# Expert weights of an MoE decoder block: pairs of ring slots filled by one load of 4 MB, and w_down split by another order of its rows

## The chip, the cores and the metric

The kernel runs on one core of a Trainium2 chip. The metric is the device time in microseconds, the median of several runs. Everything is float32.

## The reference

One decoder block over 256 tokens of width 1024. A mixer (causal pooling and sliding-window attention, each with a sigmoid gate) is followed by a mixture of experts, which takes most of the time:

```python
logits = (t @ w_router + b_router)
top_vals, top_idx = lax.top_k(logits, TOP_K)                  # 4 of 32 experts
gates = einsum('tk,tke->te', softmax(top_vals), one_hot(top_idx, 32))
for e in range(32):                                           # w_up[e]: 1024 x 2048, w_down[e]: 1024 x 1024
    hu = t @ w_up[e] + b_up[e]
    glu, lin = minimum(hu[..., ::2], 7), clip(hu[..., 1::2], -7, 7)
    act = glu * sigmoid(1.702 * glu) * (lin + 1)
    out = out + gates[:, e:e+1] * (act @ w_down[e] + b_down[e])
```

The result is x plus mixer plus experts, and one last RMSNorm. All experts are read: 32 x (8 MB + 4 MB) of weights.

## The kernel before

**Passes.** Experts are taken in pairs, 16 passes of two experts each. A pass gathers up to 64 tokens for each of its two experts by a matmul with a 0/1 matrix (`gather`, line 724, in two halves), scales them (VectorE, `copy_xg`), multiplies by w_up (line 774), applies the clamped swiglu in four pieces j of 256 columns (VectorE and ScalarE), turns the result `hid` on TensorE so that its feature dimension lies on partitions (`turn_hid`, line 761, in halves m = 0 and 1, each copied by ScalarE, `copy_hidT`, line 499), multiplies by w_down (line 819) and scatters the rows back with the gates (line 855). Overfull experts would be served by further passes at the end; there are none with these inputs.

**The ring.** All large weights pass through `ring`, ten slots of 2 MB (16 KB on each of 128 partitions). The mixer fills the first 11 places (`MIXER_LOADS`); each pass has 12 loads. Loads 0 to 7 are w_up: load 2*kk+e holds, for expert e, input features p*8+2*kk and p*8+2*kk+1 on partition p, so two matmul steps k. Loads 8 to 11 are w_down: load 8+2*m+e holds rows m*512 to m*512+511 of expert e, row m*512+p*4+c on partition p. TensorE waits for a load when it needs it (`slot_load`, line 867) and takes the kk steps in order; for kk = 0 to 2 all four output pieces j are accumulated in each step, for kk = 3 the pieces are finished one after another, so that the swiglu of piece 0 begins while TensorE is still at piece 1.

**The queue of loads.** SyncE issues all of these loads, in the order of need, one after another (lines 341 to 346). Ahead of each it waits until the slot is free (`wait_freed`, line 328): TensorE has finished the step that read the load ten places earlier. In pass 0 the first ten loads wait for the last unit of the mixer that reads the slot (`last_use`, line 326). In the last pass the last two loads are cut otherwise (by output column, into six smaller DMAs) so that the end of w_down can begin sooner.

**Order on TensorE around the turn** (`pe_pass`, line 770). After the last up matmul: `turn_hid(g, 0)`, which waits for pieces 0 and 1 of `hid`; `gather(g + 1, 0)` for the next pass; the wait for the copy of the turn; the first half of w_down (k = 0 to 3); `turn_hid(g, 1)`; `gather(g + 1, 1)`; the second half (k = 4 to 7); the bias rows of the next pass; the scatter.

Of the kernel before, what the change touches and what calls it, by code (L numbers as in the profile page):

```python
# [15 lines left out]
P = 128  # L16
D = 1024
SEQ = 256
TT = SEQ // P
KD = D // P  # L20
# [15 lines left out]
PASSES = E // 2  # L36
ROUNDS = SEQ // SLOTS - 1
LISTED = 16
NJ, CH = 4, 512
# [14 lines left out]
KK, MH = 4, 2  # L54
UP_LOADS = 2 * KK
LOADS = UP_LOADS + 2 * MH
ALL_LOADS = MIXER_LOADS + PASSES * LOADS

# [36 lines left out]
def hybrid_block_kernel(nc, x, norm1_g, w_in, pool_w, pool_scale, w_pool_proj, sinks, w_attn_proj,  # L95
# [9 lines left out]
    with ExitStack() as ctx:  # L105
# [152 lines left out]
        def load_at(n):  # L258

            return full[n % R], LANDED * (n // R + 1)  # L260
# [3 lines left out]

        def slot_of(load):

            return (MIXER_LOADS + load) % R

        block = ctx.enter_context(nc.Block())

# [2 lines left out]
        def _(sp):  # L273
# [6 lines left out]
                sp.dma_start(ring[:, n % R, :].rearrange("p (k n) -> p k n", n=D),  # L280
                             src.rearrange("(k p) n -> p k n", p=P)).then_inc(full[n % R], LANDED)

            def load_expert(slot, load, pair, split=False):

                dst = ring[:, slot, :]
                if load < UP_LOADS:
                    kk, e = load // 2, load % 2
                    src = w_up_d[bass.ds(pair * 2 + e, 1)].rearrange("e (p k) n -> p (e k n)", p=P)
                    sp.dma_start(dst, src[:, kk * SLOT:(kk + 1) * SLOT]).then_inc(full[slot], LANDED)
                elif not split or load < LOADS - 2:  # L290
                    m, e = (load - UP_LOADS) // 2, load % 2
                    src = w_down_d[bass.ds(pair * 2 + e, 1), m * CH:(m + 1) * CH, :].rearrange("e (p k) n -> p (e k n)", p=P)
                    sp.dma_start(dst, src).then_inc(full[slot], LANDED)  # L293
                else:

                    n = load - (LOADS - 2)
                    src = w_down_d[pair * 2:pair * 2 + 2, CH:2 * CH, n * CH:(n + 1) * CH].rearrange("e (p k) n -> p e k n", p=P)
                    dst = dst.rearrange("p (e k n) -> p e k n", e=2, n=CH)
                    parts = [slice(0, 4)] if n == 0 else [slice(0, 2), slice(2, 4)]
                    for i, ks in enumerate(parts):  # L300
                        for e in range(2):
                            sp.dma_start(dst[:, e, ks, :], src[:, e, ks, :]).then_inc(tail_landed[n + i], 16)

            for t in range(TT):
                sp.dma_start(acc[:, t, :], x_d[t]).then_inc(x_loaded[t], 16)
# [11 lines left out]
            for j in range(NJ):  # L317
# [10 lines left out]
            def wait_freed(g, load):  # L328

                back = load - R  # L330
# [10 lines left out]
            for g in range(PASSES):  # L341
                for load in range(LOADS):
                    if g == 0 and load < R:
                        sp.wait_ge(unit_done, UNIT[last_use[load]] + 1)
                    else:
                        wait_freed(g, load)
                    load_expert(slot_of(g * LOADS + load), load, g, split=(g == PASSES - 1))

            sp.wait_ge(extra_ready, 1)
            extras = sp.value_load(n_extra[0:1, 0:1], min_val=0, max_val=LISTED)  # L350
            with sp.If(extras > 0):
                with sp.Fori(0, extras) as t:
                    pair = sp.value_load(x_pair[0:1, bass.ds(t, 1)], min_val=0, max_val=PASSES - 1)
                    for load in range(LOADS):
                        if load < R:
                            sp.wait_ge(down_done, (t + PASSES) * MH)
                        else:
                            sp.wait_ge(up_done, (t + PASSES) * (KK - 1) + 1)
                        load_expert((ALL_LOADS + load - LOADS) % R, load, pair)
            with sp.Else():  # L360
                pass

# [178 lines left out]
        def _(pe):  # L541
# [218 lines left out]

            def turn_hid(g, m):

                pe.wait_ge(hid_ready, g * NJ + 2 * (m + 1))
                if m >= 1:
                    pe.wait_ge(hidT_copied, g * MH + m)
                for c in range(4):
                    ins = nc.tensor.transpose(turn_bank[:, c * P:(c + 1) * P], hid[:, m * CH + c:(m + 1) * CH:4], ident[:, :])  # L767
                ins.then_inc(hidT_done, 1)

            def pe_pass(g, slot_load, following, split, first):  # L770
# [6 lines left out]
                    return ins  # L777

                for kk in range(KK):
                    w = [slot_load(2 * kk + e) for e in range(2)]  # L780
# [42 lines left out]
                w = [slot_load(UP_LOADS + e).rearrange("p (k n) -> p k n", k=4) for e in range(2)]  # L823
                for k in range(4):
                    for n in range(2):
                        ins = down(k, n, [w[e][:, k, n * CH:(n + 1) * CH] for e in range(2)])
# [4 lines left out]
                    gather(g + 1, 1, gather_bank)  # L831
                pe.wait_ge(hidT_copied, g * MH + 2)
                if not split:
                    w = [slot_load(UP_LOADS + 2 + e).rearrange("p (k n) -> p k n", k=4) for e in range(2)]
                for n in range(2):
                    if split:
                        last = ring[:, slot_of(g * LOADS + LOADS - 2 + n), :].rearrange("p (e k n) -> p e k n", e=2, n=CH)
# [26 lines left out]

            def main_load(g):

                def slot_load(load):
                    pe.wait_ge(*load_at(MIXER_LOADS + g * LOADS + load))
                    return ring[:, slot_of(g * LOADS + load), :]
                return slot_load  # L870

            for g in range(PASSES):
# [4 lines left out]
            extra_slots = [(ALL_LOADS + load - LOADS) % R for load in range(LOADS)]  # L877
            with pe.If(extras > 0):
                with pe.Fori(0, extras) as t:
                    def slot_load(load):  # L880
                        slot = extra_slots[load]

                        landed = sum(n % R == slot for n in range(ALL_LOADS - 2))
                        pe.wait_ge(full[slot], t * (LANDED * extra_slots.count(slot))
                                   + LANDED * (landed + extra_slots[:load + 1].count(slot)))
# [338 lines left out]
```

## Time and profile before

| | |
|---|---|
| median of 3 runs | 1134.2 us (1133.84 to 1134.38) |
| profiled execution, its own time | 1135.42 us |
| its span, first to last instruction | 1133.6 us |
| TensorE matmul busy | 1027.0 us (91%) |
| VectorE, ScalarE busy | 251.0 us (22%), 102.4 us (9%) |
| granted TensorE clock, mean | 0.974 |
| moved by DMA | 431.55 MB, mean 381 GB/s |
| loads of w_up | 128 of 2048 KB, median 36.8 us from issue to landing |
| loads of w_down | 62 of 2048 KB, 36.8 us; in the last pass 2 of 1024 KB and 4 of 512 KB |

The DMA engines' rate is given in slices of the span. Times from issue to landing hold the time in the queue. The mixer ends at about 203 us; the rest is the 16 passes. Offsets in the trace are microseconds from the span's start.

### The profile page before, as it was taken

How to read it: one execution, taken by the hardware profiler on the slowest of the kernel's cores; microseconds unless marked ns; L12 is line 12 of the kernel's file. 1: busy time of each engine (PE TensorE's matmuls, PEld its weight loads, DVE VectorE, ACT ScalarE, POOL GpSimd, SP SyncE). 2: the span in 40 equal slices, each digit the busy share in tenths (PEclk: the TensorE clock that was granted, in tenths of full speed). 3: DMA queues.
4: the chain of work that ended last, by engine and by line, in shares of the span. 5: the costliest groups of instructions: out<-in, count | busy, mean ns of one | idle time of the engine just before them, and what ended most of it. 6: DMA issues, size and time to landing. Idle time of an engine off the chain costs nothing.

```text
span 1133.6 us, 11141 instructions
## 1 busy us (share of the span) xinstructions
PE 1027.0 (91%) x4831; PEld 480.8 (42%) x4831; DVE 251.0 (22%) x561; ACT 102.4 (9%) x226; POOL 8.9 (1%) x20
## 2 busy tenths in 40 slices
PE   5499999999999998989898998898998989898986
PEld 4388874543434342424242434243434333333332
DVE  2032112331313211203031212121212121212112
ACT  1032011200101000001010101000000000000002
POOL 1200000000000000000000000000000000000000
PEclk9799999899999999999999999999999999999999
DMA  8760794699999999999999999999999999999994
GB/s 246 199 230 1 263 429 171 264 429 427 427 428 427 428 428 426 428 430 427 428 427 429 425 429 428 426 430 427 426 430 426 427 429 427 428 428 426 429 422 173
DMA packets 43302, 431.55 MB, mean 381 GB/s; under 512 B 5479, under 2 KB 7196, under 8 KB 18932
## 3 DMA queue, kind: packets, MB, share of 16 engines
q1 hardware_dynamic: 39992, 427.58, 89.7%
q0 software_dynamic: 976, 2.63, 1.4%
q10 hardware_dynamic: 2284, 0.60, 0.2%
q8 instruction: 40, 0.66, 0.2%
q14 instruction: 10, 0.08, 0.0%
HBM read 428.17 MB, written 2.62 MB: 380 GB/s over the span
## 4 chain that ended last, share of the span: by engine, by line
PE 51%; DMA 47%; DVE 1%; SPq 1%; issue 0%; ACT 0%; DVEq 0%; ACTq 0%
DMA ring<-in_w_down 32%; PE bank L774 15%; PE bank L819 15%; DMA ring<-in_w_up 11%; PE bank L572 9%; DMA ring<-in_w_in 4%; PE bank L729 3%; PE bank L855 3%; PE bank L675 3%; PE bank L767 1%; PE bank L758 1%; PE bank L692 0%; PE bank L589 0%; SPq L293 0%; PE bank L615 0%
## 5 line engine op out<-in xcount | busy, mean ns | idle before, releaser
L774 PE MATMUL bank<-ring,z_buf 128*64 128x512 f32 x2048 | 466.8, 610 | 51.0 <-issue 28.0
L774 PEld LDWEIGHTS bank<-ring,z_buf 128*64 128x64 f32 x2048 | 155.6, 140 | 347.7 <-issue 347.7
L819 PE MATMUL bank<-ring,m_buf 128*64 128x512 f32 x1024 | 226.8, 595 | 9.7 <-DMA ring<-in_w_down 9.0
L819 PEld LDWEIGHTS bank<-ring,m_buf 128*64 128x64 f32 x1024 | 78.1, 137 | 135.3 <-issue 132.7
L572 PE MATMUL bank<-h_buf,ring 128*128 128x256 f32 x400 | 91.5, 385 | 16.5 <-DMA ring<-in_w_in 15.6
L1116 DVE TENSOR_SCALAR swi<-bank 128x256 f32<-128x256 f32 x64 | 27.2, 425 | 311.9 <-PE bank L774 306.9
L572 PEld LDWEIGHTS bank<-h_buf,ring 128*128 128x128 f32 x400 | 76.7, 193 | 28.0 <-DMA ring<-in_w_in 16.1
L729 PE MATMUL bank<-u_buf,h_buf 128*128 128x128 f32 x512 | 64.5, 281 | 0.1
L729 PEld LDWEIGHTS bank<-u_buf,h_buf 128*128 128x128 f32 x512 | 62.1, 198 | 0.2 <-issue 0.2
L510 ACT ACTIVATE swi<-swi 128x256 f32<-128x256 f32 x64 | 26.7, 417 | 389.1 <-DVE swi L1116 389.1
L855 PE MATMUL bank<-y,u_buf 128*128 128x512 f32 x128 | 59.2, 605 | 0.0
L1087 DVE TENSOR_TENSOR z_buf<-bank,g2x 128x512 f32<-128x512 f32 x32 | 22.1, 692 | 148.5 <-PE bank L729 148.5
L1092 DVE TENSOR_TENSOR acc<-acc,bank 128x512 f32<-128x512 f32 x64 | 44.0, 687 | 30.0 <-PE bank L855 30.0
L855 PEld LDWEIGHTS bank<-y,u_buf 128*128 128x128 f32 x128 | 23.0, 189 | 35.1 <-issue 35.1
L1127 DVE COPY y<-bank 128x512 f32<-128x512 f32 x16 | 11.1, 692 | 113.8 <-PE bank L819 113.8
L501 ACT COPY m_buf<-bank 128x512 f32<-128x512 f32 x32 | 18.5, 577 | 143.6 <-PE bank L767 143.6
L675 PE MATMUL bank<-ring,m_buf 128*128 128x512 f32 x64 | 29.1, 615 | 0.0
L767 PEld LDWEIGHTS bank<-ident,m_buf 128*128 128x128 f32 x128 | 17.8, 209 | 26.0 <-issue 26.0
L497 ACT COPY u_buf<-bank 128x256 f32<-128x256 f32 x16 | 6.0, 372 | 243.7 <-PE bank L737 243.7
L1122 DVE TENSOR_TENSOR m_buf<-swi 128x256 f32<-128x256 f32 x64 | 27.2, 425 | 2.4
L1119 DVE SCALAR_TENSOR_TENSOR swi<-swi 128x256 f32<-128x256 f32 x64 | 27.2, 425 | 2.2
L1117 DVE TENSOR_SCALAR swi<-bank 128x256 f32<-128x256 f32 x64 | 26.6, 415 | 0.0
(169 smaller groups left out, 322.1 us busy)
## 6 DMA issues: line engine op xcount, KB each, us to landing
ring<-in_w_up SPq DMA_DIRECT2D x128, 2048.0 KB, 36.8
ring<-in_w_down SPq DMA_DIRECT2D x62, 2048.0 KB, 36.8
ring<-in_w_in SPq DMA_DIRECT2D x6, 2048.0 KB, 31.6
ring<-in_w_out SPq DMA_DIRECT2D x2, 2048.0 KB, 15.7
ring<-in_w_pool_proj SPq DMA_DIRECT2D x1, 2048.0 KB, 21.8
ring<-in_w_attn_proj SPq DMA_DIRECT2D x1, 2048.0 KB, 22.4
ring<-in_w_down SPq DMA_DIRECT2D x2, 1024.0 KB, 32.8
ring<-in_w_down SPq DMA_DIRECT2D x4, 512.0 KB, 11.0
```

The lines of the kernel that those rows point to most:

```text
L510: nc.scalar.activation(sig, glu, ACT.Sigmoid, scale=ALPHA).then_inc(sigmoid_ready, 1)
L572: ins = nc.tensor.matmul(dst, w[:, k, c * P:(c + 1) * P], rhs[:, k, :], start=(k == 0), stop=(k == kn - 1))
L675: ins = nc.tensor.matmul(b[:, :], mixedT[:, k, t * P:(t + 1) * P], w[:, k % 4, n * CH:(n + 1) * CH], start=(k == 0), stop=(k == KD - 1))
L729: ins = nc.tensor.matmul(b[:, k * P:(k + 1) * P], x1r[:, t, (4 * half + k) * P:(4 * half + k + 1) * P], pick[:, t, :], start=(t == 0), sto ...
L767: ins = nc.tensor.transpose(turn_bank[:, c * P:(c + 1) * P], hid[:, m * CH + c:(m + 1) * CH:4], ident[:, :])
L774: ins = nc.tensor.matmul(up_banks[j][e * SLOTS:(e + 1) * SLOTS, :], xgT[:, k, e * SLOTS:(e + 1) * SLOTS], w[e].rearrange("p (k n) -> p k n ...
L819: ins = nc.tensor.matmul(down_banks[n][e * SLOTS:(e + 1) * SLOTS, :], hidT[:, k, e * SLOTS:(e + 1) * SLOTS], w[e], start=(k == 0), stop=(k ...
L855: nc.tensor.matmul(scatter_banks[q][:, :], spreadT[:, t * P:(t + 1) * P], y[:, n * CH:(n + 1) * CH], start=True, stop=True).then_inc(scatt ...
L1092: nc.vector.tensor_tensor(acc[:, t, n * CH:(n + 1) * CH], acc[:, t, n * CH:(n + 1) * CH], scatter_banks[q][:, :], ALU.add).then_inc(added, 1)
L1116: nc.vector.tensor_scalar(glu, pairs[:, :, 0], LIMIT, None, ALU.min).then_inc(glu_ready, 1)
L1119: nc.vector.scalar_tensor_tensor(lin, lin, 1.0, glu, ALU.add, ALU.mult).then_inc(gated_ready, 1)
L1122: nc.vector.tensor_tensor(hid[:, j * CF:(j + 1) * CF], lin, sig, ALU.mult).then_inc(hid_ready, 1)
```

## The change

Three things are changed.

- **Places.** The loads of a pass are numbered so that neighbours belong together: w_up of expert e, step kk, is at `4*(kk//2) + 2*e + kk%2`, w_down of expert e, half m, at `8 + 2*e + m`. One place of the ring is skipped behind the mixer (`FIRST`), so that even places fall on even slots. In passes 1 to 14 one DMA fills two neighbouring slots: 4 MB, 32 KB on each partition, six DMAs a pass. It waits until both slots are free, and TensorE waits for the whole of it. In passes 0 and 15 the loads stay single, 2 MB each, issued in the order of need (with load 9 of pass 0 moved ahead of load 7, since its slot is free earlier). TensorE's steps keep their order.
- **w_down.** Partition p holds rows p*8 to p*8+7 of an expert's w_down instead of p*4+c of each half. So `turn_hid(g, m)` takes columns 4*m+c, c+8, ... of `hid`, which are spread over all four pieces, and both turns wait for all of them.
- **Order.** The gather of the next pass's first half stands ahead of the first turn.

The core of the diff (the counts of landed loads and the code for further passes are left out):

```diff
+FIRST = MIXER_LOADS + 1
+ALL_LOADS = FIRST + PASSES * LOADS
+def up_place(kk, e):
+    return 4 * (kk // 2) + 2 * e + kk % 2
+def down_place(m, e):
+    return UP_LOADS + 2 * e + m
...
-            def load_expert(slot, load, pair, split=False):
...
+            def load_expert(slot, i, pair, wide):
+                dst = ring[:, slot, :] if wide == 1 else ring[:, slot:slot + 2, :].rearrange("p s n -> p (s n)")
+                e = (i // 2) % 2
+                if i < UP_LOADS:
                     src = w_up_d[bass.ds(pair * 2 + e, 1)].rearrange("e (p k) n -> p (e k n)", p=P)
...
+                    kk = 2 * (i // 4) + i % 2
+                    sp.dma_start(dst, src[:, kk * SLOT:(kk + wide) * SLOT]).then_inc(full[slot], LANDED)
+                elif wide == 1:
+                    m = i % 2
+                    src = w_down_d[bass.ds(pair * 2 + e, 1)].rearrange("e (p k) n -> p (e k n)", p=P)
+                    sp.dma_start(dst, src[:, m * SLOT:(m + 1) * SLOT]).then_inc(full[slot], LANDED)
+                else:
+                    src = w_down_d[bass.ds(pair * 2 + e, 1)].rearrange("e (p k) n -> p (e k n)", p=P)
                     sp.dma_start(dst, src).then_inc(full[slot], LANDED)
...
-            last_use = ["gate_pool1", "q1", "gate_pool5", "gate_pool7", "gate_attn1", "gate_attn7",
-                        "gate_attn5", "gate_attn7", "out3", "out3"]
+            last_use = ["q1", "gate_pool5", "gate_pool7", "gate_attn1", "gate_attn7", "gate_attn5",
+                        "gate_attn7", "out3", "out3", "gate_pool1"]
+            def wait_freed(g, i):
+                back = i - R
                 if back < 0:
                     back, g = back + LOADS, g - 1
-                kk, m = back // 2, (back - UP_LOADS) // 2
+                kk = 2 * (back // 4) + back % 2
                 if back >= UP_LOADS:
-                    sp.wait_ge(down_done, MH * g + m + 1)
+                    sp.wait_ge(down_done, MH * g + back % 2 + 1)
...
+            by_need = [up_place(kk, e) for kk in range(KK) for e in range(2)]
+            for i in by_need[:7] + [9, by_need[7], 8]:
+                sp.wait_ge(unit_done, UNIT[last_use[i]] + 1)
+                load_expert(slot_of(i), i, 0, 1)
+            for i in (10, 11):
+                wait_freed(0, i)
+                load_expert(slot_of(i), i, 0, 1)
+            for g in range(1, PASSES - 1):
+                for i in range(0, LOADS, 2):
+                    wait_freed(g, i)
+                    wait_freed(g, i + 1)
+                    load_expert(slot_of(g * LOADS + i), i, g, 2)
+            for i in by_need + [down_place(0, e) for e in range(2)]:
+                wait_freed(PASSES - 1, i)
+                load_expert(slot_of((PASSES - 1) * LOADS + i), i, PASSES - 1, 1)
+            for n in range(2):
+                wait_freed(PASSES - 1, TAIL[n])
+                load_tail(PASSES - 1, n)
...
             def turn_hid(g, m):
 
-                pe.wait_ge(hid_ready, g * NJ + 2 * (m + 1))
+                pe.wait_ge(hid_ready, (g + 1) * NJ)
...
-                    ins = nc.tensor.transpose(turn_bank[:, c * P:(c + 1) * P], hid[:, m * CH + c:(m + 1) * CH:4], ident[:, :])
+                    ins = nc.tensor.transpose(turn_bank[:, c * P:(c + 1) * P], hid[:, 4 * m + c:D:KD], ident[:, :])
...
-                turn_hid(g, 0)
                 if following:
                     gather(g + 1, 0, gather_bank)
+                turn_hid(g, 0)
```

## Rows read from the trace of the kernel before

**Rows 1.** The page: GB/s moved in 40 slices of 28.3 us; the chain's shares by engine.

```profile
GB/s 246 199 230 1 263 429 171 264 429 427 427 428 427 428 428 426 428 430 427 428 427 429 425 429 428 426 430 427 426 430 426 427 429 427 428 428 426 429 422 173
...
PE 51%; DMA 47%; DVE 1%; SPq 1%; issue 0%; ACT 0%; DVEq 0%; ACTq 0%
```

**Rows 2.** PE's timeline, passes 5 and 6: start, us, line, count, idle before and releaser.

```profile
516.34 7.09 PE L819 MATMUL bank<-ring,m_buf 128*64 128x512 f32 x32 [0.25 <-DMA ring<-in_w_down]
...
526.13 7.09 PE L819 MATMUL bank<-ring,m_buf 128*64 128x512 f32 x32 [0.24 <-DMA ring<-in_w_down]
...
555.44 8.78 PE L774 MATMUL bank<-ring,z_buf 128*64 128x512 f32 x32 [2.36 <-issue]
```

**Rows 3.** PE's timeline, pass 1 and the start of pass 2.

```profile
294.14 7.09 PE L819 MATMUL bank<-ring,m_buf 128*64 128x512 f32 x32
...
303.62 7.09 PE L819 MATMUL bank<-ring,m_buf 128*64 128x512 f32 x32
...
315.34 7.09 PE L774 MATMUL bank<-ring,z_buf 128*64 128x512 f32 x32
...
343.48 0.75 PE L767 MATMUL bank<-ident,m_buf 128*128 128x128 f32 x4
...
345.94 7.09 PE L819 MATMUL bank<-ring,m_buf 128*64 128x512 f32 x32
```

**Rows 4.** SyncE's timeline, from the second half of the mixer to pass 1.

```profile
121.54 1.01 SPq L276 DMA_DIRECT2D ring<-in_w_in  x2
...
196.21 21.66 SPq L293 DMA_DIRECT2D ring<-in_w_down  x4
...
224.66 25.61 SPq L289 DMA_DIRECT2D ring<-in_w_up  x8
...
258.95 12.52 SPq L293 DMA_DIRECT2D ring<-in_w_down  x4
...
278.06 24.02 SPq L289 DMA_DIRECT2D ring<-in_w_up  x8
```

**Rows 5.** The ring's loads issued from 200 to 330 us: duration, first and last start; landing.

```profile
L293 SPq DMA_DIRECT2D ring<-in_w_down x10: 327/380/433, 217.1 to 322.8; - x10
...
DMA to landing us min/median/max: 7.7/19.8/27.4
```

**Rows 6.** Timeline of all engines at the end of up, pass 0.

```profile
239.88 0.75 PE L767 MATMUL bank<-ident,m_buf 128*128 128x128 f32 x4
...
241.53 0.42 DVE L1122 TENSOR_TENSOR m_buf<-swi 128x256 f32<-128x256 f32 x1
```

**Rows 7.** PE in the last passes (timeline), then the chain: start, us, what.

```profile
1057.82 7.09 PE L819 MATMUL bank<-ring,m_buf 128*64 128x512 f32 x32 [0.24 <-DMA ring<-in_w_down]
...
1106.81 7.09 PE L819 MATMUL bank<-ring,m_buf 128*64 128x512 f32 x32 [2.08 <-DMA ring<-in_w_down]
...
1113.89 0.69 PE bank L767 x4
...
1115.25 7.09 PE bank L819 x32
```

**Rows 8.** DMA issues from 120 to 145 us; then w_in's and w_out's issues and landings.

```profile
ring<-in_w_in SPq DMA_DIRECT2D x1, 2048.0 KB, 7.6
...
ring<-in_w_in SPq DMA_DIRECT2D x1, 1024.0 KB, 10.1
...
L276 SPq DMA_DIRECT2D ring<-in_w_in x7: 384/781/32876, 2.8 to 122.0; - x7
...
L280 SPq DMA_DIRECT2D ring<-in_w_out x2: 1277/2074/2872, 122.6 to 125.5; - x2
...
DMA to landing us min/median/max: 14.6/15.7/16.8
```

**Rows 9.** Windows: busy us of each engine, clock, DMA share, GB/s (last).

```profile
130.00:132.00 2.00, 2.00 (x11) 1.77 (x10) 0.00 (x0) 0.00 (x0) 0.00 (x0) 1.00 1.10 364
...
132.50:142.00 9.50, 9.50 (x45) 8.36 (x45) 1.69 (x4) 0.38 (x1) 0.00 (x0) 1.00 1.05 420
```

More of the change, by code:

```diff
@@ L56, with in_pairs, count_landed @@
 LOADS = UP_LOADS + 2 * MH
-ALL_LOADS = MIXER_LOADS + PASSES * LOADS
+FIRST = MIXER_LOADS + 1
[4 more added lines that the diff above has]
+    return UP_LOADS + 2 * e + m
+def in_pairs(g):
+    return 0 < g < PASSES - 1
+TAIL = [down_place(1, e) for e in range(2)]
+def count_landed():
+    loads = [0] * R
+    for n in range(MIXER_LOADS):
+        loads[n % R] += 1
+    at = {}
+    for g in range(PASSES):
+        for i in range(LOADS):
+            if g == PASSES - 1 and i in TAIL:
+                continue
+            slot = (FIRST + g * LOADS + i) % R
+            if in_pairs(g) and i % 2:
+                at[g, i] = at[g, i - 1]
+            else:
+                loads[slot] += 1
+                at[g, i] = slot, loads[slot]
+    return at, loads
+LANDED_AT, LANDED_LOADS = count_landed()
 UNITS = ([("vectors", "dve"), ("bias_rows", "dve")]
@@ L265, in slot_of @@
         def slot_of(load):
-            return (MIXER_LOADS + load) % R
+            return (FIRST + load) % R
         block = ctx.enter_context(nc.Block())
@@ L281, in load_rows @@
                              src.rearrange("(k p) n -> p k n", p=P)).then_inc(full[n % R], LANDED)
-            def load_expert(slot, load, pair, split=False):
-                dst = ring[:, slot, :]
-                if load < UP_LOADS:
-                    kk, e = load // 2, load % 2
+            def load_expert(slot, i, pair, wide):
+                dst = ring[:, slot, :] if wide == 1 else ring[:, slot:slot + 2, :].rearrange("p s n -> p (s n)")
+                e = (i // 2) % 2
+                if i < UP_LOADS:
@@ L288, in load_expert @@
                     src = w_up_d[bass.ds(pair * 2 + e, 1)].rearrange("e (p k) n -> p (e k n)", p=P)
[L289 to L292, printed above, removed]
-                    sp.dma_start(dst, src).then_inc(full[slot], LANDED)
[L294 to L302, printed above, removed]
+                    kk = 2 * (i // 4) + i % 2
@@ new lines, in load_expert @@
+                    sp.dma_start(dst, src[:, kk * SLOT:(kk + wide) * SLOT]).then_inc(full[slot], LANDED)
[3 more added lines that the diff above has]
+                    sp.dma_start(dst, src[:, m * SLOT:(m + 1) * SLOT]).then_inc(full[slot], LANDED)
+                else:
+                    src = w_down_d[bass.ds(pair * 2 + e, 1)].rearrange("e (p k) n -> p (e k n)", p=P)
+                    sp.dma_start(dst, src).then_inc(full[slot], LANDED)
@@ new lines, in load_tail @@
+            def load_tail(g, n):
+                src = w_down_d[2 * g:2 * g + 2].rearrange("e (p k) n -> p e k n", p=P)[:, :, KD // 2:, n * CH:(n + 1) * CH]
+                dst = ring[:, slot_of(g * LOADS + TAIL[n]), :].rearrange("p (e k n) -> p e k n", e=2, n=CH)
+                parts = [slice(0, 4)] if n == 0 else [slice(0, 2), slice(2, 4)]
+                for i, ks in enumerate(parts):
+                    for e in range(2):
+                        sp.dma_start(dst[:, e, ks, :], src[:, e, ks, :]).then_inc(tail_landed[n + i], 16)
@@ L339, in wait_freed @@
                     sp.wait_ge(up_done, (KK - 1) * g + kk + 1)
[L341 to L347, printed above, removed]
+            by_need = [up_place(kk, e) for kk in range(KK) for e in range(2)]
[16 more added lines that the diff above has]
+                load_tail(PASSES - 1, n)
             sp.wait_ge(extra_ready, 1)
@@ L353, in _ @@
                     pair = sp.value_load(x_pair[0:1, bass.ds(t, 1)], min_val=0, max_val=PASSES - 1)
-                    for load in range(LOADS):
-                        if load < R:
+                    for i in by_need + [down_place(m, e) for m in range(MH) for e in range(2)]:
+                        if i < R:
                             sp.wait_ge(down_done, (t + PASSES) * MH)
                         else:
-                            sp.wait_ge(up_done, (t + PASSES) * (KK - 1) + 1)
-                        load_expert((ALL_LOADS + load - LOADS) % R, load, pair)
+                            sp.wait_ge(up_done, (t + PASSES) * (KK - 1) + 2)
+                        load_expert((ALL_LOADS + i - LOADS) % R, i, pair, 1)
             with sp.Else():
@@ L779, in pe_pass @@
                 for kk in range(KK):
-                    w = [slot_load(2 * kk + e) for e in range(2)]
+                    w = [slot_load(up_place(kk, e)) for e in range(2)]
                     if kk % 2 == 0:
@@ L821, in down @@
                     return ins
-                w = [slot_load(UP_LOADS + e).rearrange("p (k n) -> p k n", k=4) for e in range(2)]
+                w = [slot_load(down_place(0, e)).rearrange("p (k n) -> p k n", k=4) for e in range(2)]
                 for k in range(4):
@@ L833, in pe_pass @@
                 if not split:
-                    w = [slot_load(UP_LOADS + 2 + e).rearrange("p (k n) -> p k n", k=4) for e in range(2)]
+                    w = [slot_load(down_place(1, e)).rearrange("p (k n) -> p k n", k=4) for e in range(2)]
                 for n in range(2):
                     if split:
-                        last = ring[:, slot_of(g * LOADS + LOADS - 2 + n), :].rearrange("p (e k n) -> p e k n", e=2, n=CH)
+                        last = ring[:, slot_of(g * LOADS + TAIL[n]), :].rearrange("p (e k n) -> p e k n", e=2, n=CH)
                     for k in range(4, 8):
@@ L865, in main_load, with slot_load @@
             def main_load(g):
-                def slot_load(load):
-                    pe.wait_ge(*load_at(MIXER_LOADS + g * LOADS + load))
-                    return ring[:, slot_of(g * LOADS + load), :]
+                def slot_load(i):
+                    slot, loads = LANDED_AT[g, i]
+                    pe.wait_ge(full[slot], LANDED * loads)
+                    return ring[:, slot_of(g * LOADS + i), :]
                 return slot_load
@@ L876, in _, with slot_load @@
             extras = pe.value_load(n_extra[0:1, 0:1], min_val=0, max_val=LISTED)
-            extra_slots = [(ALL_LOADS + load - LOADS) % R for load in range(LOADS)]
+            extra_slots = [(ALL_LOADS + i - LOADS) % R for i in range(LOADS)]
             with pe.If(extras > 0):
                 with pe.Fori(0, extras) as t:
-                    def slot_load(load):
-                        slot = extra_slots[load]
-                        landed = sum(n % R == slot for n in range(ALL_LOADS - 2))
+                    def slot_load(i):
+                        slot = extra_slots[i]
                         pe.wait_ge(full[slot], t * (LANDED * extra_slots.count(slot))
-                                   + LANDED * (landed + extra_slots[:load + 1].count(slot)))
+                                   + LANDED * (LANDED_LOADS[slot] + extra_slots[:i + 1].count(slot)))
                         return ring[:, slot, :]
```

2 lines of the change are left out of this document (removed).

## The prediction

> **What bounds the kernel now.** I read the page's rate by slice and its chain first. From slice 9 to the one before last the DMA engines move 422 to 430 GB/s without a pause, and the chain is half TensorE, half transfers into the ring [rows 1]. Then TensorE's timeline in a late pass: it stands still for 2.36 us ahead of an up step (put down to issue, but all its other work is there), and halves 0 and 1 of w_down start at 516.34 and 526.13, 9.79 us apart for two loads, so 4.9 us a load [rows 2]. Twelve loads are 58.8 us. In an early pass the same engine waits for nothing [rows 3]: up 28.14 (315.34 to 343.48), turn and gather 2.46 (to 345.94), first half of w_down with the next turn and gather 9.48 (294.14 to 303.62), second half with bias rows and scatter 11.72 (303.62 to 315.34); together 51.8 us. So the MoE part is a stream of loads, and only three things can move the end: a stop in the stream after it has become continuous, the pace of the stream, and what TensorE still has to do when the last loads land.
>
> SyncE's issues show where the stream becomes continuous. They come at 196.21 (slots of the output projection), at 217.1 (the first two loads of pass 0 used) and at 224.66 [rows 4, 5]. By 217.1 ten loads of pass 0 are in or on their way in either kernel, so what counts is the stream from 217.1 on. A load issued into a dry queue lands 7.7 us later at the least [rows 5], against 4.9 after its predecessor in a full one: a stop costs 2.8 us on top of the wait.
>
> **Issue of pass 0 and pass 1 (order and pairs).** What changes before 217.1 is harmless. The changed order puts three instead of four loads ahead of the wait for gate_attn1, and a free slot's load behind gate_attn7; the queue may be dry for some us around 160, but the eight loads before the wait for out3 land by about 186, and the next ones can't be issued before 196.21. Cost 0 (up to 1). From 217.1:
> - Load 10 lands at 217.1 + 7.6 = 224.7. Before, load 11 was released by the same event and landed 4.9 later. Now it sits on the slot of an up load of kk=1, free at 224.66; it lands at 224.66 + 7.6 = 232.3 instead of 229.6: 2.7 lost.
> - Pass 1's first wide load follows, to 242.0. The second needs kk 2 and 3 of pass 0, free at the end of up, about 239.95; from a dry queue 4 MB land 7.7 + 4.8 = 12.5 after the issue, at 252.5, against 251.7 in a full one: 0.8 lost.
> - The fourth needs both halves of w_down of pass 0, 258.95 before [rows 4], 1.1 later now (below): 260.1 + 12.5 = 272.6 against 271.9: 0.6 lost.
> - The sixth needs kk=1 of pass 1: about 279.2 + 12.5 = 291.7 against 292: nothing. After that TensorE gains 6 us a pass on the stream, and no wait for a slot is late.
> Sum 4.1 us, bounds 2.7 (only the first, which is plain) and 6.7 (2.7 and twice the 2.0 that a stop leaves with the least overlap).
>
> **Steady passes.** With pairs the stream brings up 0-1, up 2-3 and down in groups of 8 MB, 19.5 us each. Let down land at 0. TensorE: 0.14 + 9.48 + 11.72 = 21.3, so up 0-1 (landed at 19.5) starts 1.8 late and ends at 35.8 (14.4 of the 28.14); it waits 3.2 for up 2-3 at 39; 13.8 more and the turn (below) give about 56.4, 2 ahead of the next down at 58.4. Slots: a wide load takes the pair that was filled five wide loads before it. The one that must start at 48.7 takes up 0-1's, free at 35.8; the one that starts at 87.7 takes down's, free at 58.4 + 16.6 = 75. These two are the tightest, 12.7 us and more ahead, against 2.8 of a restart. So the queue stays full and each pass is paced by bytes: 0. A wait of 2.36 us has been followed by a slow group, 8.78 instead of 7.09 us [rows 2]; after a wait of 3.2 that may come in each pass, and its 1.7 us fits in the 5 us of slack.
>
> **The turn.** Before, the first turn needed only columns of the first two swiglu pieces. Now both need all four. On TensorE up ends at 239.88; the last piece of hid starts at 241.53 and takes 0.42 [rows 6], so hid is ready 2.07 after up. The gather, moved ahead, fills 1.9 of it. Then the turn and its copy by ScalarE (m_buf) stand open: from the start of a turn to the matmul behind its copy 1.36 us (1113.89 to 1115.25) [rows 7]. Up to down is 2.07 + 0.1 + 1.36 = 3.5 instead of 2.46, +1.1 a pass. In passes 1 to 14 it is hidden under the wait for w_down; in pass 0 it is the 1.1 used above. The gather's copy by VectorE comes no later: VectorE reaches it behind the last piece of hid in either order.
>
> **The last pass.** This is where the pairing is paid once more. Counting from the landing of the last w_down load of pass 14: before, that load was the second half, and TensorE began it at 1057.82; ten loads later, at 1106.81, it began the last pass's first half, after a wait of 2.08 [rows 7]. That is 49.0. Now the first half starts there too, since both come in one load: 0.14 + 9.48 + 11.72 + 28.14 + 3.5 (no gather here, the turn waits open) = 53.0, without any wait for the single loads, which come in 49. The end behind it is the same in both kernels. Cost 53.0 - 49.1 = 3.9 us; bounds 3.7 and 5.6 (one slow group of +1.7 on this stretch).
>
> **The pace.** The new thing is rows of 32 KB, half the packets. The trace has rows of three sizes in full queues. From issue plus time to landing [rows 8]: w_in's load of 2 MB 121.54 + 7.6 = 129.1, its 1 MB load with 1 KB rows 122.0 + 10.1 = 132.1, w_out 122.6 + 14.6 = 137.2 and 125.5 + 16.8 = 142.3 with 4 KB rows. So 1 MB with 64 packets an engine took 3.0, 2 MB with 32 packets 5.1, and 2 MB with 8 packets 4.9. Twice the first less the last is 6.0 - 4.9 = 1.1 us for 128 - 8 = 120 packets, 9.2 ns each; the second pair gives 0.2 / 24 = 8.3. Windows give less [rows 9]: 16 KB on one engine take 262,144 / 364 = 720 ns at 1 KB rows, 624 at 4 KB, and 612 at the 428 GB/s of 16 KB rows [rows 1], so 7.2 ns and 3.9 ns a packet. I take 9.2, from the landings, since windows split packets at their ends. A wide load saves 8 packets an engine, 74 ns; 84 of them save 6.2 us. Bounds 0 (rows above 16 KB stand nowhere in the trace) and 12.4: without any cost by packet a load takes 4.9 - 8 x 0.0092 = 4.82, so 168 x 0.074.
>
> The Trainium skill (DMA: Bandwidth & Descriptors, "Where 436 GB/s comes from") puts the ports' ceiling at 435.2 GB/s. 4.82 us for 2 MB is just that, so page and rows agree on the asymptote. The same page ("Why small descriptors are slow") names a fixed cost of about 3 cycles a packet, some 3.5 ns at that port rate: the estimate by it would be 84 x 8 x 3.5 ns = 2.4 us saved, near rival A.
>
> The same page, "Anatomy of one DMA", charges a DMA a fixed 2 us, so that fewer and larger DMAs would save 2 us each. In this stream it is not so: landings 4.9 us apart with a restart of 7.7 show that cost only when the queue is dry, and 84 fewer issues are worth nothing by themselves.
>
> SyncE issues 84 fewer DMAs of 0.33 us; it sits waiting for slots between them: 0.
>
> **Sum.** 4.1 + 3.9 - 6.2 = +1.8, and I round to +2 for the small openings after copies. The profiled execution took 1135.4 (span 1133.6 and 1.8 around it); it becomes 1137.4. The median of the runs is 1.2 below the profiled one: 1136.2.
>
> **Rivals.**
> - A, the packets save less than the landings say: 3.9 ns a packet, the 4 KB window's price, gives 84 x 8 x 3.9 ns = 2.6 saved, net +5.4, 1139.6. If rows of 32 KB go out as two packets, nothing is saved: +8, 1142.2. For it: no row above 16 KB in the trace. Against: the landings of three sizes lie on one line, though each is read to 0.1 us only, 1 to 2 ns a packet. It decides once the saving is under 5.7 us (8.5 ns a packet); then the kernel is slower beyond what can be told. Chance 0.33.
> - B, larger packets reach the port's full rate: 12.4 saved, net -4.4, 1129.8. For it: the rate is 1.6% under the asymptote. Against: the cost goes by packets. Chance 0.08.
> - C, the start or the tail is cheaper than counted (pass 0's later releases are overlapped, TensorE catches up in the last pass): 2.7 + 1.5 - 6.2 = -2, 1132.2, down to -4. Against: nothing in the last pass can be skipped. Chance 0.1.
> - D, the pairs starve the queue in each pass: the tightest slot comes free 12 us ahead; would it come under 2.8, each us lost is paid 13 times, +13 for 1 us, 1149. It decides if TensorE's pass grows by 9 us. Against: slack of 5 us a pass. Chance 0.04.
> - The forecast's own case, +0.5 to +3.5: 0.45.
>
> What can be told from no change here is 0.2%, 2.3 us. A (0.33), D (0.04) and the forecast's upper part (0.06) give slower 0.43; B, and half of C that passes -2.3, give faster 0.13; the rest, 0.44, is the same. The range 1131.5 to 1141 leaves out D, B and the extreme of A.
>
> **What would show it.** Right: the rate in passes 2 to 13 at about 431 GB/s instead of 428, groups of w_down 58.4 us apart; a short dip of the rate between 222 and 227; in the last pass no wait of TensorE for a load from its start to the end of up, then some 3.5 us to w_down. Wrong: a rate of 428 (A) or 434 (B), dips in each pass (D), a wait for w_down in the last pass (C).

## The result and the profile after

The changed kernel takes 1138.89 us (median of 20 runs, 1133.77 to 1140.75), the kernel before beside it 1134.59 (20 runs, 1133.64 to 1136.28). The ratio is 1.0033, 95% interval 1.0025 to 1.0040: 3.8 us slower, where 2.0 were forecast. The ratio goes by all runs and agrees with the means, which are 3.8 us apart; the medians are 4.3 apart. A second comparison, on another chip, gave 1.0031 (1.0019 to 1.0043). The profiled execution took 1136.2, its span 1134.5, so it is 2.7 us faster than the median; the second comparison left a trace too (1137.92, span 1136.2), which is nearer to it.

The page of the changed kernel, its rate by slice, the granted clock and the chain by engine, and its issues of loads:

```profile
PEclk9899999999999999989999999989999999999998
...
GB/s 247 216 211 1 292 376 251 251 409 423 438 429 430 433 430 430 432 431 430 433 430 432 432 430 428 433 432 428 433 432 428 434 430 430 430 432 427 425 405 72
...
PE 71%; DMA 25%; DVE 2%; issue 1%; ACT 1%; SPq 0%; DVEq 0%; ACTq 0%
...
ring<-in_w_up SPq DMA_DIRECT2D x56, 4096.0 KB, 24.7
ring<-in_w_down SPq DMA_DIRECT2D x28, 4096.0 KB, 24.0
```

Against [rows 1] the stream is faster in the middle and thinner at both ends (409 and 423 where it starts, 405 and 72 where it stops), and the chain has moved from half transfers to TensorE. Part of the thin end is that this execution's stream ran out earlier (the mixer, below). The queue of the loads, before and then after (packets, MB, share of 16 engines):

```profile
q1 hardware_dynamic: 39992, 427.58, 89.7%
```

```profile
q1 hardware_dynamic: 27896, 427.58, 88.9%
```

12,096 packets fewer are 84 x 16 x 9. So a row of 32 KB is one packet, and a wide load saves nine packets on each engine and not eight: eight of rows, and one small one that every DMA brings for itself (4 bytes in the packet records, 9 ns). A window of the middle (columns as in [rows 9]), the kernel before, then the changed one:

```profile
300.00:1000.00 700.00, 644.02 (x3028) 259.31 (x3026) 146.92 (x313) 44.80 (x97) 0.00 (x0) 0.98 1.01 428
```

```profile
300.00:1000.00 700.00, 645.03 (x2982) 256.49 (x2982) 146.91 (x312) 44.98 (x95) 0.00 (x0) 0.97 1.00 431
```

431 was forecast. 32 KB on one engine take 2 x 262,144 / 428 = 1225 ns as two packets and 1216 as one: 8.5 ns a packet, to some 3 ns, since each rate is rounded to 1 GB/s. From the packet records of the two traces the rates are 427.6 and 430.9, which makes it 9.4.

**The start.** SyncE's timeline of the changed kernel, the counterpart of [rows 4]:

```profile
193.02 27.41 SPq L334 DMA_DIRECT2D ring<-in_w_down  x3
220.54 35.24 SPq L330 DMA_DIRECT2D ring<-in_w_up  x4
255.87 19.01 SPq L337 DMA_DIRECT2D ring<-in_w_down  x2
274.98 33.53 SPq L330 DMA_DIRECT2D ring<-in_w_up  x4
```

```profile
L334 SPq DMA_DIRECT2D ring<-in_w_down x2: 327/328/328, 212.5 to 220.1; - x2
```

In the second fence (the ring's loads issued from 200 to 290 us) load 10 of pass 0 goes out at 212.5 and load 11 at 220.1, 7.6 later, where both stood at 217.1 and 217.4 before. The rates of this time are shown with the experiment on the start. In this execution the mixer happened to end early: pass 0's first weights were used by 212.5, against 217.1 [rows 5]. That is 4.6 us of luck, and it has to be taken off when the two traces are compared. (The changed kernel's second trace has 216.5; the traces of both kernels and the variants lie between 211.9 and 217.1.)

**The end.** TensorE's timeline of the changed kernel from w_down of pass 14 on, the counterpart of [rows 7]:

```profile
1051.56 8.78 PE L875 MATMUL bank<-ring,m_buf 128*64 128x512 f32 x32 [2.87 <-DMA ring<-in_w_down]
...
1062.70 7.09 PE L875 MATMUL bank<-ring,m_buf 128*64 128x512 f32 x32
...
1074.42 7.09 PE L830 MATMUL bank<-ring,z_buf 128*64 128x512 f32 x32
...
1081.81 20.82 PE L830 MATMUL bank<-ring,z_buf 128*64 128x512 f32 x96
1104.67 0.71 PE L823 MATMUL bank<-ident,m_buf 128*128 128x128 f32 x4 [2.05 <-DVE m_buf L1177]
1106.06 8.78 PE L875 MATMUL bank<-ring,m_buf 128*64 128x512 f32 x32 [0.68 <-ACT m_buf L557]
...
1116.16 7.09 PE L875 MATMUL bank<-ring,m_buf 128*64 128x512 f32 x32 [0.68 <-ACT m_buf L557]
```

From 1051.56 to 1102.6 TensorE waits for no load; then it rests 2.05 us for hid and 0.68 for the copy, as the sum had it (1102.63 to 1106.06 is 3.43, forecast 3.5). But two groups of 32 matmuls take 8.78 us instead of 7.09: part of each ran at a granted clock of about 0.5, the lower of the two levels (1.2 GHz), each right behind a rest. Two windows in them (the clock stands before the last two columns):

```profile
1052.00:1055.00 3.00, 3.00 (x10) 1.17 (x8) 0.00 (x0) 0.00 (x0) 0.00 (x0) 0.50 0.96 410
1107.00:1109.00 2.00, 2.00 (x7) 0.49 (x5) 0.00 (x0) 0.00 (x0) 0.00 (x0) 0.50 0.58 226
```

**The ledger of the two traces.** From pass 0's first weights used to the first half of w_down of pass 14 in the changed kernel: 1051.56 - 212.5 = 839.1; to the second half in the kernel before: 1057.82 - 217.1 = 840.7. So -1.6, where the sum had +4.1 - 6.2 = -2.1. From there to the end of the span: 1134.5 - 1051.6 = 82.9 against 1133.6 - 1057.8 = 75.8: +7.1, where the sum had 3.9. With the mixer's -4.6 this is +0.9, the difference of the two spans. Without it, it is +5.5 in this pair of executions, and 3.8 by the ratio of all runs.

**The second trace of the changed kernel** is nearer to that. Its TensorE timeline in passes 14 and 15:

```profile
1035.49 15.65 PE L830 MATMUL bank<-ring,z_buf 128*64 128x512 f32 x64 [3.18 <-issue]
...
1054.97 7.09 PE L875 MATMUL bank<-ring,m_buf 128*64 128x512 f32 x32 [1.16 <-DMA ring<-in_w_down]
...
1107.77 8.78 PE L875 MATMUL bank<-ring,m_buf 128*64 128x512 f32 x32 [0.67 <-ACT m_buf L557]
```

Here 1054.97 - 216.5 = 838.5, which is -2.2 against 840.7, where the sum had -2.1. From there to the end 1136.2 - 1055.0 = 81.2, +5.4: from w_down to w_down 52.8 against 49.0, so +3.8 where the sum had +3.9, and one slow group, +1.7. Together +3.2.

What differs between the two traces is where pass 14's slow stretch stood. The first trace had in the same pass:

```profile
1032.07 13.96 PE L830 MATMUL bank<-ring,z_buf 128*64 128x512 f32 x64 [1.48 <-issue]
```

In both traces each pass from 3 to 14 has one slow stretch, in one of two places. Either it stands behind the wait for the second half of up (64 matmuls in 15.65 us instead of 13.95), and the wait for w_down behind it is only 1.15 us and full speed follows; or up runs at full speed, TensorE waits 2.85 us for w_down, and the slow group is that of w_down. The first trace has it in up in passes 3 to 9 and in w_down in passes 10 to 14, the second one has both kinds as well and ends with it in up. In a steady pass both are hidden; in pass 14 the one in up is hidden and the one in w_down is paid, 1.7 us.

### The profile page after: what moved, and what is told of

It is laid out like the page before. It is cut to its first block, busy times and chain, and to the rows that moved or that the text cites. A ratio compares the mean times of both kernels' runs of the same rounds, so it can differ in the third digit from the quotient of the medians.

```text
span 1134.5 us, 11141 instructions
## 1 busy us (share of the span) xinstructions
PE 1035.3 (91%) x4831; PEld 480.3 (42%) x4831; DVE 250.9 (22%) x561; ACT 104.2 (9%) x226; POOL 8.9 (1%) x20
## 3 DMA queue, kind: packets, MB, share of 16 engines
q1 hardware_dynamic: 27896, 427.58, 88.9%
## 4 chain that ended last, share of the span: by engine, by line
PE 71%; DMA 25%; DVE 2%; issue 1%; ACT 1%; SPq 0%; DVEq 0%; ACTq 0%
PE bank L830 25%; DMA ring<-in_w_down 21%; PE bank L875 21%; PE bank L628 9%; PE bank L911 5%; DMA ring<-in_w_in 4%; PE bank L785 3%; PE bank L731 2%; PE bank L814 2%; PE bank L823 1%; PE bank L793 1%; PE bank L748 0%; PE bank L645 0%; ACT m_buf L557 0%; DVE m_buf L1177 0%
## 5 line engine op out<-in xcount | busy, mean ns | idle before, releaser
L875 PE MATMUL bank<-ring,m_buf 128*64 128x512 f32 x1024 | 237.7, 619 | 27.0 <-DMA ring<-in_w_down 23.0
L823 PE MATMUL bank<-ident,m_buf 128*128 128x128 f32 x128 | 22.7, 300 | 2.1 <-DVE m_buf L1177 2.0
```

The source lines that it names most:

```text
L875: ins = nc.tensor.matmul(down_banks[n][e * SLOTS:(e + 1) * SLOTS, :], hidT[:, k, e * SLOTS:(e + 1) * SLOTS], w[e], start=(k == 0), stop=(k ...
```

## The experiments

All ratios are to the kernel before on the same chip, with 95% intervals. The runs were spread over three chips, and a step from one ratio to another is known to 1.3 to 2.3 us only. Where a text below says "off the change", it is the step from 1.0033.

**Packets at the changed kernel's schedule.** Each wide load is issued as two, TensorE waits for both:

```diff
-                    load_expert(slot_of(g * LOADS + i), i, g, 2)
+                    load_expert(slot_of(g * LOADS + i), i, g, 1)
+                    load_expert(slot_of(g * LOADS + i + 1), i + 1, g, 1)
```

> The changed kernel with each load of 4 MB issued as two loads of 2 MB (rows of 16 KB), behind the same two waits, and TensorE waiting for both. Only the size of a packet differs. If a packet costs 9.2 ns (my theory), 84 x 8 x 9.2 ns = 6.2 us slower than the changed kernel: about 1145, landings of a pair 9.79 us apart instead of 9.71. If it costs 3.9 ns (rival A), 2.6 us slower: 1141.5. If the gain of rows of 32 KB is something else than the count of packets, no difference: 1139.

Measured 1144.47 (6 runs, 1140.39 to 1147.82), ratio 1.0094 (1.0076 to 1.0113): 0.0061 above the changed kernel's 1.0033, some 6.9 us (4.7 to 9.2). The rate in the middle:

```profile
300.00:1000.00 700.00, 641.09 (x2966) 254.03 (x2967) 146.79 (x312) 45.33 (x96) 0.00 (x0) 0.96 1.01 427
```

Back at 427 with the order, the waits and the slots of the change. The gain comes from the wide loads; rival A (2.6 us) and rival B (12.4 us) both fall. The expectation says that only the size of a packet differs, which isn't quite so: there are 84 DMAs more as well, and the queue is back at the 39,992 packets of before.

**Packets at the schedule of before.** Each expert load of 2 MB becomes two of 1 MB with rows of 8 KB:

```diff
-                    sp.dma_start(dst, src).then_inc(full[slot], LANDED)
+                    for h in range(2):
+                        sp.dma_start(dst[:, h * HALF:(h + 1) * HALF], src[:, h * HALF:(h + 1) * HALF]).then_inc(full[slot], LANDED)
```

> The kernel before with each expert load of 2 MB issued as two DMAs of 1 MB whose rows are 8 KB: twice the packets, the schedule as it was. 180 loads stand in the continuous stream. At 9.2 ns a packet and some 2 to 9 ns for the second DMA's own descriptor: 180 x 76 to 83 ns = 14 to 15 us slower, 1149. At 3.9 ns: 6 to 7 us, 1141. If a DMA has a cost of its own in a full queue, more than 15.

Measured 1146.32 (4 runs), 1.0115 (1.0100 to 1.0130): 13 us (11.3 to 14.7) for 180 loads of 8 more packets of rows an engine and one DMA more, 72 ns a load. That is 9 ns a packet if the DMA itself costs nothing, and 8 if its small packet costs as much as the others. The middle runs at 421 GB/s:

```profile
300.00:1000.00 700.00, 635.68 (x2966) 254.88 (x2962) 146.10 (x311) 43.64 (x95) 0.00 (x0) 0.98 1.01 421
```

So 8, 16 and 32 KB rows run at 421, 428 and 431 GB/s, and the line of the landings [rows 8] holds from 1 KB to 32 KB (by unrounded rates 9.5 ns a packet here, 9.4 between 16 and 32 KB). Both runs change rows and DMAs together, so they don't separate the price of a row from that of a DMA; what they leave for the second DMA, beside 8 packets at 9.2, is next to nothing.

**The end alone.** Pass 14 is loaded singly too:

```diff
-    return 0 < g < PASSES - 1
+    return 0 < g < PASSES - 2
...
+            for i in by_need + [down_place(m, e) for m in range(MH) for e in range(2)]:
+                wait_freed(PASSES - 2, i)
+                load_expert(slot_of((PASSES - 2) * LOADS + i), i, PASSES - 2, 1)
```

> The changed kernel with pass 14 loaded singly as well, in the order of need (pairs in passes 1 to 13). If the end is lengthened by the pairing of pass 14 (TensorE starts w_down 9.5 us later against the stream), the last pass again waits for its single loads: 3.9 us less, and the two slow groups at the end (3.4 us) go or become one; 0.4 us of packets lost: 1132 to 1134. If the end has another cause (the turn that waits for all of hid), little changes: 1138 or more.

Measured 1134.89 (12 runs, 1129.71 to 1136.45), 1.0002 (0.9990 to 1.0014): 3.5 us off the change (1.9 to 5.1), where 4.9 to 6.9 were expected. Its last pass, TensorE's timeline:

```profile
1093.66 7.09 PE L833 MATMUL bank<-ring,z_buf 128*64 128x512 f32 x32 [0.15 <-DMA ring<-in_w_up]
1102.79 0.71 PE L826 MATMUL bank<-ident,m_buf 128*128 128x128 f32 x4 [2.04 <-DVE m_buf L1180]
1104.17 10.10 PE L878 MATMUL bank<-ring,m_buf 128*64 128x512 f32 x32 [0.68 <-ACT m_buf L560]
```

TensorE has just caught the stream again (a wait of 0.15), since pass 14 had started behind pass 13's pair; and the slow group still stands behind the rest for hid and loses 3.0 us here. From pass 0's first weights (215.6 here) the first half of w_down of pass 14 starts at 835.4 us, against 838.5 in the second trace of the changed kernel. So the lag is a cause; how much of the 3.5 us is lag and how much a slow group of pass 14, this run doesn't separate. The rest of the turn stays.

**Start and end.** In addition pass 1 is loaded singly, with the loads of pass 0 and 1 nearly in the order in which their slots come free:

```diff
-            for i in (10, 11):
-                wait_freed(0, i)
-                load_expert(slot_of(i), i, 0, 1)
+            for g, i in [(0, 10), (1, 0), (0, 11), (1, 2), (1, 1)] + [(1, i) for i in by_need[3:] + [8, 10, 9, 11]]:
+                wait_freed(g, i)
+                load_expert(slot_of(g * LOADS + i), i, g, 1)
```

> As the last one, and passes 1 too is loaded singly, each load issued in the order in which its slot comes free: load 10 of pass 0, load 0 of pass 1, load 11 of pass 0, and so on. My sum says that the order at the start costs 4.1 us; 72 wide loads are left (0.4 us less gain). So 3.6 us faster than the kernel with pass 14 single: 1129 to 1130, 5 below the kernel before. If the start is overlapped anyway (rival C), no more than 1 us faster.

Measured 1131.49 (12 runs), 0.9985 (0.9974 to 0.9997): 1.9 us off the kernel above by the ratios, 3.4 by the medians, where 3.6 were expected; the interval of the step, 0 to 3.8, holds both. My order had two slips: load 2 of pass 1 stands ahead of load 1 though its slot is freed later, and load 10 ahead of load 9. I put each at a stop of some 0.7 us. In the trace the rate falls to 350 and 371 GB/s in the windows from 230 to 236 us and to 300 and 371 in those from 272 to 278; against 428 that is some 2 us for both.

**The start alone**, with that order mended (1, 2 and 8, 9, 10, 11), pairs in passes 2 to 14 and the end as in the changed kernel:

> The changed kernel with the start alone mended: pass 1 is loaded singly, and the loads of passes 0 and 1 are issued in the order in which their slots come free (pairs in passes 2 to 14, the end as in the changed kernel). The stops of 3.9 us in the stream behind pass 0 go, 0.4 us of packets is lost: 3.5 us faster than the changed kernel, 0.2 below to level with the kernel before (1.0000 to 1.0005). If the stops are overlapped by other waits (rival C), 1.003 as the changed kernel.

Measured 1134.93 (12 runs), 1.0003 (0.9994 to 1.0012): 3.4 us off the change (2.1 to 4.7), and 3.2 below the changed kernel on the same chip (1.0031, last experiment), as expected. The profiled execution is the fastest of the twelve, 1129.97: its mixer ended early (211.9), and it has no slow group in its last pass. Windows of 3 us behind pass 0's first weights, the changed kernel and then this one (both have that moment at about 212 us):

```profile
214.00:217.00 3.00, 3.00 (x18) 1.00 (x16) 0.00 (x0) 0.00 (x0) 0.00 (x0) 1.00 0.86 366
217.00:220.00 3.00, 3.00 (x18) 0.76 (x14) 0.00 (x0) 0.00 (x0) 0.00 (x0) 1.00 0.61 262
220.00:223.00 3.00, 3.00 (x22) 1.21 (x22) 1.41 (x4) 0.00 (x0) 0.00 (x0) 1.00 0.63 208
223.00:226.00 3.00, 3.00 (x17) 1.00 (x14) 0.00 (x0) 0.00 (x0) 0.00 (x0) 1.00 0.99 426
```

```profile
214.00:217.00 3.00, 3.00 (x16) 1.01 (x14) 0.00 (x0) 0.00 (x0) 0.00 (x0) 1.00 1.01 431
217.00:220.00 3.00, 3.00 (x20) 0.89 (x16) 0.00 (x0) 0.00 (x0) 0.00 (x0) 1.00 1.02 437
220.00:223.00 3.00, 3.00 (x18) 1.06 (x16) 1.42 (x4) 0.00 (x0) 0.00 (x0) 1.00 0.99 426
```

The stop of load 11 is the hole of 262 and 208, the dip forecast for 222 to 227, some 4.6 us earlier with this execution's mixer: 3 x (366 + 262 + 208) against 3 x (431 + 437 + 426) is 1.4 MB, 3.2 us at 428 GB/s.

**The turn alone.** The kernel before with w_down as f = p*8+k, both turns behind all of hid and the gather first, no pairs (the lines of `turn_hid` and `pe_pass` as in the change):

> The kernel before with the second and third part of the change alone: w_down as f = p*8+k, both turns behind all of hid, the gather ahead of the first turn; no pairs. The stream stays as it was. Up to down grows by 1.1 us a pass, hidden in all passes but the last. There the up matmuls end at 1104 and w_down starts 3.5 us later instead of with its load's landing at 1106.8: 0.7 us, 1134.4. If TensorE's rest of 2 + 0.7 us around the turn also brings a stretch of half clock (1.7 to 3.0 us, as the traces of the changed kernel and of the kernel with pass 14 single show in the last pass), 1136 to 1137.5.

Measured 1134.23 (11 runs), 1.0004 (0.9996 to 1.0013): the first branch, no slow group. Its end on TensorE's timeline:

```profile
1104.47 0.71 PE L767 MATMUL bank<-ident,m_buf 128*128 128x128 f32 x4 [2.04 <-DVE m_buf L1122]
1105.85 7.09 PE L819 MATMUL bank<-ring,m_buf 128*64 128x512 f32 x32 [0.68 <-ACT m_buf L501]
```

The same rests of 2.04 and 0.68, and full speed behind them. So the rests alone don't bring the slow group each time. By themselves parts two and three cost nothing that can be told: 0.5 us, at most 1.5.

**Rests filled.** The changed kernel with two spare matmuls ahead of the last pass's first turn, and two in pass 14 behind it:

```diff
+            def keep_busy():
+                nc.tensor.matmul(up_banks[0][:, :], ident[:, :], x1r[:, 0, 0:CH], start=True, stop=True, skip_group_check=True)
...
+                if split:
+                    pe.wait_ge(hid_ready, g * NJ + 1)
+                    keep_busy()
+                    keep_busy()
                 turn_hid(g, 0)
+                if isinstance(g, int) and g in (PASSES - 2,):
+                    keep_busy()
+                    keep_busy()
```

> The changed kernel with spare matmuls of 128x512 that go nowhere: two in the last pass while TensorE waits for hid, two in pass 14 while it waits for w_down. If the two slow groups at the end (8.78 instead of 7.09 us each) come from these rests, they go: 3.4 us faster than the changed kernel where both stood, some 2 us in the median, 1.0015 of the kernel before, and a narrower spread. If they don't come from the rests, the same time as the changed kernel or 1 us more, 1.0033 and up.

Measured 1135.94 (12 runs, 1132.57 to 1138.33), 1.0019 (1.0007 to 1.0030), 1.6 us off the change (0 to 3.1). The trace has the lag without the slow groups:

```profile
1082.67 20.82 PE L834 MATMUL bank<-ring,z_buf 128*64 128x512 f32 x96
1105.55 0.71 PE L823 MATMUL bank<-ident,m_buf 128*128 128x128 f32 x4
1106.94 7.09 PE L886 MATMUL bank<-ring,m_buf 128*64 128x512 f32 x32 [0.68 <-ACT m_buf L557]
```

The interval overlaps the changed kernel's (1.0025 to 1.0040), and the spread isn't narrower, so this supports the clock's part in the cost and doesn't settle its size. One trace says little here: in this one pass 14's slow stretch stood in up (64 matmuls in 15.65 us), so that its w_down would likely have run at full speed without the spare matmuls too, as in the changed kernel's second trace, and the traces of the start alone and of the pairs taken apart have no slow group behind the last turn either, with nothing filled.

**The same in the kernel with passes 0, 1 and 14 single** (only the two matmuls of the last pass):

> The kernel with passes 0, 1 and 14 single, plus two such matmuls in the last pass during the wait for hid. It had a slow group of 8.67 us there (1.6 us lost), and its neighbour one of 10.10 (3.0 lost). If the rest brings it: 1.5 us faster than that kernel in the median, 0.997 of the kernel before. Else no difference, 0.9985.

Measured 1131.46 (12 runs), 0.9981 (0.9970 to 0.9992): no difference that can be told from 0.9985. In its trace a slow group stands one step earlier, behind a rest of 2.76 us for a load, where nothing was filled:

```profile
1094.55 8.78 PE L837 MATMUL bank<-ring,z_buf 128*64 128x512 f32 x32 [2.76 <-DMA ring<-in_w_up]
```

A slow group that is avoided in one place can turn up in the next; this run tells nothing more.

**A version better than both.** Pairs in passes 2 to 13; the single passes keep the split of w_down and the turn of the kernel before; the loads of passes 0 and 1 in the order of freeing:

```diff
-    return 0 < g < PASSES - 1
+    return 1 < g < PASSES - 2
...
-                pe.wait_ge(hid_ready, (g + 1) * NJ)
+                wide = isinstance(g, int) and in_pairs(g)
+                pe.wait_ge(hid_ready, (g + 1) * NJ if wide else g * NJ + 2 * (m + 1))
...
+                if not wide:
+                    turn_hid(g, 0)
                 if following:
                     gather(g + 1, 0, gather_bank)
-                turn_hid(g, 0)
+                if wide:
+                    turn_hid(g, 0)
```

> Pairs in passes 2 to 13 only; in all passes loaded singly w_down is split as before and the turn stands as before; loads of passes 0 and 1 in the order in which slots come free (the two stops of 0.7 us left in that stream mended). By the terms: 72 wide loads save 5.3 us, nothing is lost at the start or in the last pass: 5.3 us below the kernel before, 0.9953. If the last pass still runs behind the stream, 2 us less.

Measured 1129.69 (5 runs, 1129.23 to 1131.20), 0.9964 (0.9951 to 0.9977). And again:

> The same kernel as the best so far, for a narrower interval: 0.9953 by the terms of the sum, 0.9964 as measured from five executions.

1129.87 (5 runs), 0.9952 (0.9939 to 0.9965): 4 to 5.4 us faster than the kernel before, where the terms said 5.3. The last pass waits for its loads again:

```profile
1100.52 8.78 PE L884 MATMUL bank<-ring,m_buf 128*64 128x512 f32 x32 [2.32 <-DMA ring<-in_w_down]
```

**The changed kernel again**, beside the last ones:

> The changed kernel itself beside these, on one chip: 1.003 to 1.004 of the kernel before.

1138.03 (6 runs), 1.0031 (1.0019 to 1.0043).

## Why the prediction was right, and where it was short

- **What bounds the kernel: right.** The stream of loads does. All terms that were forecast are terms of the stream or of what follows it, and they add up within the intervals, at the very edge for the kernel with pass 14 single, which gained 3.5 us (at most 5.1) where 4.9 at the least were expected.
- **Start, 4.1 us: right.** Mending it alone gave 3.4 us with 0.4 of packets lost, so 3.8, to 1.3 us. The largest part is the stop of load 11, seen as a hole in the rate. Rival C falls for this part.
- **Pace, -6.2 us: right.** 8.5 ns a packet by the windows, 9.4 by unrounded rates, where 9.2 was forecast; taking the pairs apart again costs 6.9 us back. The estimate of 3.5 ns a packet in the prediction falls with rival A. The window's 3.9 ns, on which rival A stood, was a poor reading of a short window: single packets took 161 ns with 4 KB and 614 with 16 KB (medians of the trace before), so (4 x 161 - 614) / 3 = 10 ns.
- **Steady passes, 0: right.** The rate holds 425 to 434 GB/s from slice 12 to 38, so no pass starves; rival D falls. The first halves of w_down start 58.3 us apart in most passes (58.4 forecast) and about 60 in three of twelve. TensorE's slow stretches there are hidden, but not for the reason given: behind the wait for up there are not 5 us of slack, only the 2 ahead of w_down. With 1.7 us lost the wait for w_down is 1.15, of which 0.68 is the copy's, so it just fits. A stretch that loses 2.4 us or more, behind a longer wait for up (4.70), doesn't fit, and w_down starts late.
- **The turn, 1.1 us a pass and hidden: right.** 3.43 us from up to w_down; alone it moves nothing that can be told (1.0004).
- **Last pass, 3.9 us: the mechanism right, the term too small.** It measured 7.1 in the profiled pair and 5.4 in the second trace. The lag of 3.9 is there to a tenth (1051.56 to 1106.06 is 54.5, less one slow group's 1.7 is 52.8, and 52.8 in the second trace; forecast 53.0). It is taken from 49.0, as read; the 49.1 in the sum is a slip. On top stand two slow groups of 1.7 us each in the first trace, one in pass 14 and one behind the turn of the last pass, and only the last pass's in the second. I had one of them as the upper bound and none in the sum. I argued that 1.7 us fits in the slack of a steady pass, and it does; but pass 14's w_down group is the first of a stretch with no slack at all, and its rest of 2.87 us is of the size that had been followed by a slow group before [rows 2]. With one such group in the sum the forecast would have been 1137.9. The ratio, 3.8 against the 2.0 forecast, asks for about one of them. That the sum came out within 2 us is no luck of terms that cancel: start, pace and lag each measured what was forecast, to the precision of the runs.

What stays open is what decides whether a slow group follows a rest: behind rests of 2.04 and 0.68 us in the last pass three traces have none (the turn alone, the start alone, the pairs taken apart) and four lose 1.7, 1.7, 3.0 and 1.6 us (both of the changed kernel, pass 14 single, passes 0, 1 and 14 single). For the same reason the spread of the changed kernel, 7.0 us against 2.6 before, is explained in part only.

## What to carry to other kernels

When a kernel is a stream of loads, ask of a change only three things: does the stream stop after it has become continuous, what is its pace, and what is left when it ends. Coarser loads help the pace in the middle and cost at both ends, since slots are released and data handed over in larger lumps; so use them only where work on both sides has slack, and keep single loads where the stream starts and where it runs out. When the tail gets a stretch without slack, count the slow stretches of TensorE that were free before.

## What the runs showed of the hardware

- A row of 32 KB on a partition goes out as one packet: 27,896 packets in the queue instead of 39,992. Each DMA brings one small packet more on each engine. Rates in a full queue on one core: 421 GB/s for 8 KB rows, 428 for 16 KB, 431 for 32 KB, 8.5 to 9.5 ns a packet on an engine.
- Two DMAs instead of one for the same bytes, with rows half as long, cost 72 ns a load in a full queue, which eight packets at 9 ns account for. Into a dry queue a load of 2 MB lands 7.1 us later at the least, against 4.9 in a full one.
- In the changed kernel TensorE rests twice a pass, for up and for w_down, and from pass 3 on the granted clock fell to the lower level once a pass, behind the one rest (3.2 us) or the other (2.85): 1.7 us lost as a rule, 2.4 to 3.0 now and then. Which of the two it is changes within one execution.
- With spare matmuls in a rest of 2 us one kernel's tail had no slow group in its trace, and in another the slow group stood behind another rest. Whether the spare matmuls did it, one trace each doesn't show.
